# Headwise products as multiply-adds in a new channel order, and the gates of three pairs by seven products, in an mLSTM and latent-attention step

## The chip, the cores and the metric

One core of one Trainium2 chip runs the whole program. The metric is device microseconds of one execution. TensorE, VectorE (DVE), ScalarE (ACT) and GpSimd (POOL) work beside each other on SBUF and PSUM; SyncE (SP) issues nearly all DMA transfers from one queue. Everything is float32. A float32 matmul appears in the trace as two records, a transpose by the identity as one.

## What is computed

Two layers over 640 frames (512 of a new prompt, and 16 of each of 8 running streams), width 1024. The first is an mLSTM layer with 2048 channels in 4 heads of 512; the second is multi-head latent attention with 8 heads. The part that the change touches:

```python
def headwise(x, w):                       # w: 512 groups of 4 x 4
    xb = x.reshape(B, T, -1, QKV_BLOCK)
    return jnp.einsum('btgi,gio->btgo', xb, w).reshape(B, T, -1)

u = rmsnorm(x, norm_w) @ w_in             # mlstm_layer
x_in, z = u[..., :MLSTM_INNER], u[..., MLSTM_INNER:]
xc = jax.nn.silu(causal_conv(x_in, buf, conv_w, conv_b)[0])
q, k, v = headwise(xc, w_q), headwise(xc, w_k), headwise(x_in, w_v)
g = (q @ w_gates[:MLSTM_INNER] + k @ w_gates[MLSTM_INNER:2 * MLSTM_INNER]
     + v @ w_gates[2 * MLSTM_INNER:] + b_gates)
...
u = rmsnorm(x, norm_w) @ w_in             # mla_layer
gate = u[..., Q_LORA_RANK:]               # 8 tiles of 128 channels
return x + (o * jax.nn.silu(gate)) @ w_out
```

Each headwise product mixes only four neighbouring channels. Per head, k of a frame is weighed, and new states C (512 x 512) and n are formed for the prompt and for each of the 8 streams; all are outputs.

## The kernel before

**Layout.** Activations stand with channels on partitions and frames along the free dimension: a tile is 128 channels x 640 frames, an mLSTM head is four tiles (`KH`). Weights come through a ring of four slots, `ring`, 512 KB each.

**Stage A** (about 28 to 297 us) goes over the 16 channel tiles n. For each, TensorE forms x and z of the tile from the 8 tiles of the normalised input. From tile 2 on this is done by seven products in place of eight: the weights and the tokens are split in quarters, GpSimd forms four sums or differences of weights (`mixed_weights`, L2515 to L2520, 128x512 each), and the partial products are added up by VectorE (`finish_x`, `finish_z`, `middle_sums`, `lower_right`, `upper_left`) and ScalarE (`p1_kept`). TensorE works one tile ahead: while VectorE and ScalarE do the causal conv of tile n (`tap0` on ScalarE, three multiply-add taps on VectorE at L1941 and L1944) and ScalarE's SiLU, TensorE does the last z product of tile n and the products of tile n+1.

Between these products, `to_tokens` (L758) multiplies five blocks of 128 frames of x, and later of the conv's output, by a 128 x 136 matrix `basis`: 128 columns of block-diagonal 4 x 4 weights, built by GpSimd from `bdmask` (`basis_tile`), and 8 columns of gate weights. The result has frames on partitions: v from x, k from the conv's output, and the tile's share of the 8 gate rows. VectorE copies v and k out of PSUM (L1962) and adds the gates up in `gacc` (L1970); SP stores v, k and z of each tile to scratch in HBM (320 KB each). GpSimd copies the conv's output into `xc` (L2538).

**Gate rows** (about 297 to 323 us). TensorE transposes `gacc` (L869); ScalarE and VectorE form log-sigmoid, the running sums and maxima on four rows, and TensorE broadcasts the first head's row (`broadcast_first_m`, L907). Beside that, TensorE forms k and q of head 0 with channels on partitions by block-diagonal matmuls (`project_keys` L888, `project_queries` L875), and the score products (`scores`, L936) of the query blocks t = 0, 1 ahead of the broadcast and 2 to 4 behind it. SP issues four loads of old states (1024 KB each) and then, when everything stored is there (`scratch_written`), v and k of head 0.

**Heads** (about 324 to 575 us). For each head, prompt values (`prompt_values`, L1013), the stream states in eight steps (`step`: products in four column groups at L989, outer products at L1004, which VectorE adds to the old states in `update`, L2149), the prompt's new state (`prompt_c`, L1037), transposes of the normalised output (`turn`, L1022). VectorE takes statistics (`statistics`, L2122 to L2141), GpSimd the inverse roots. After step 6 of a head, `project_head` (L875, L888) forms q and k of the next, then comes step 7 and the next head's scores. ScalarE weighs k in place for the state update (`weigh_k`, L1575).

**Attention pairs** (760 to 1029 us). Four pairs of heads. While scores, maxima, exponentials and transposes go round between the engines, TensorE fills its gaps (`filler`) with the gate products of the next pair, in the first three pairs: two gate tiles of 8 k-tiles x 2 halves, 32 matmuls of 320 columns a pair (`gate_tiles`, L708).

Each engine has its own instruction stream, and the order is written out by hand; a wait names a semaphore and a count. SP's queue is in order too: a DMA behind a waiting one waits with it.

## Time and profile before

| | |
|---|---|
| median of 3 runs | 1047.45 us (1046.79 to 1049.26) |
| the profiled execution | 1046.36 us, its span 1044.6 us |
| TensorE busy | 1019.8 us (98%), 4334 matmul records |
| VectorE, ScalarE, GpSimd busy | 503.3, 259.6, 271.1 us |
| chain that ended last | TensorE 63% of the span, VectorE 4% |
| DMA | 164.20 MB, one queue, 42.5% of 16 engines' span |
| mean granted TensorE clock | 0.998 of full speed |

The span runs from the first to the last instruction; the device time is some 1.8 us longer. Matmuls are pipelined, so that the duration of one is longer than the distance from one start to the next; distances between starts are the better price. L numbers are lines of the kernel before.

### The profile page before, as it was taken

The page shows a single profiled execution, that of the slowest core. Times are in us where ns is not written, and L with a number is a line of the kernel's source. Part 1 is how long each engine was busy: PE and PEld are TensorE (multiplying, and loading weights), DVE is VectorE, ACT ScalarE, POOL GpSimd, SP SyncE. Part 2 cuts the span into 40 slices and gives each one's busy share as a digit, 9 for nine tenths or more (in the row PEclk, how much of TensorE's full clock was granted, in tenths as well). Part 3 has the DMA queues.
Part 4 walks back from the last instruction along what each step waited for, and adds up shares of the span by engine and source line. Part 5 has one row for each costly group of instructions (what it writes and reads, how often), then busy time and mean ns, then how long its engine had stood idle before and what let it go on. Part 6 is the DMA issues. An engine that isn't in the chain of part 4 may idle for free.

```text
span 1044.6 us, 12018 instructions
## 1 busy us (share of the span) xinstructions
PE 1019.8 (98%) x4334; PEld 654.8 (63%) x4334; DVE 503.3 (48%) x1134; ACT 259.6 (25%) x541; POOL 271.1 (26%) x345
## 2 busy tenths in 40 slices
PE   7999999999989999999999999999999999999998
PEld 4777777777755453444535777777766666655665
DVE  5964444444466566685665532244233333344224
ACT  3222121212154242232431000011222323243221
POOL 3552525252313234142132063311110101010110
PEclk9999999999999999999999999999999999999999
DMA  7224232423375989979798322112210111203202
GB/s 269 78 99 157 92 109 112 156 90 110 111 298 179 397 323 346 373 302 391 300 374 332 146 81 81 55 46 104 92 64 20 63 41 44 88 31 127 79 27 101
DMA packets 44464, 164.20 MB, mean 157 GB/s; under 512 B 4916, under 2 KB 8248, under 8 KB 35456
## 3 DMA queue, kind: packets, MB, share of 16 engines
q1 hardware_dynamic: 44416, 163.56, 42.5%
q8 instruction: 30, 0.49, 0.2%
q14 instruction: 18, 0.15, 0.0%
HBM read 106.32 MB, written 57.23 MB: 157 GB/s over the span
## 4 chain that ended last, share of the span: by engine, by line
PE 63%; DVE 4%; DMA 1%; POOL 1%; ACT 1%; issue 1%; SPq 0%; POOLq 0%; ACTq 0%
PE work_b L708 11%; PE work_a L708 7%; PE work_b L1246 5%; PE work_a L1037 5%; PE bank L1121 5%; PE work_a L936 3%; PE bank L1004 2%; PE work_b L1121 2%; PE work_b L989 2%; DVE arena L2149 2%; PE bank L1291 2%; PE work_a L1316 2%; PE work_a L1276 1%; PE bank L1425 1%; PE work_a L1121 1%; PE work_a L1013 1%
## 5 line engine op out<-in xcount | busy, mean ns | idle before, releaser
L2149 DVE SCALAR_TENSOR_TENSOR arena<-arena,bank 128x512 f32<-128x512 f32 x128 | 87.0, 742 | 59.3 <-PE bank L1004 59.3
L708 PE MATMUL work_b<-arena,ring 128*128 128x320 f32 x384 | 107.8, 433 | 0.0
L708 PEld LDWEIGHTS work_b<-arena,ring 128*128 128x128 f32 x384 | 71.5, 190 | 27.7
L1037 PE MATMUL work_a<-arena 128*128 128x512 f32 x128 | 64.1, 613 | 2.7 <-ACT arena L1581 2.7
L813 PE MATMUL work_a<-arena 128*128 128x320 f32 x224 | 64.9, 433 | 0.4 <-DVE arena L1916 0.4
L813 PE MATMUL work_a<-arena,ring 128*128 128x320 f32 x224 | 64.9, 432 | 0.0
L813 PE MATMUL work_b<-arena 128*128 128x320 f32 x224 | 62.7, 432 | 0.0
L708 PE MATMUL work_a<-arena,ring 128*128 128x320 f32 x192 | 55.4, 449 | 7.2 <-DMA ring<-in_stream 7.2
L2659 POOL COPY arena<-arena 32x640 f32<-32x640 f32 x20 | 16.6, 832 | 163.0 <-ACT arena L1696 156.7
L813 PEld LDWEIGHTS work_b<-arena 128*128 128x128 f32 x224 | 42.6, 190 | 17.7
L708 PEld LDWEIGHTS work_a<-arena,ring 128*128 128x128 f32 x192 | 37.9, 198 | 23.2 <-DMA ring<-in_stream 7.2
L813 PEld LDWEIGHTS work_a<-arena 128*128 128x128 f32 x224 | 41.5, 190 | 16.1 <-issue 0.6
L813 PEld LDWEIGHTS work_a<-arena,ring 128*128 128x128 f32 x224 | 41.5, 190 | 15.5
L1463 ACT ACTIVATE arena<-arena 128x128 f32<-128x128 f32 x16 | 5.0, 314 | 167.9 <-DVE arena L1876 150.4
L2581 POOL TENSOR_TENSOR xc<-arena 128x2048 f32<-128x2048 f32 (+1 forms) x8 | 23.2, 2900 | 89.4 <-DVE arena L2169 89.4
L758 PEld LDWEIGHTS bank<-arena 128*128 128x128 f32 x320 | 41.6, 190 | 7.0 <-ACT arena L1489 2.1
L758 PE MATMUL bank<-arena 128*128 (+1 forms) x320 | 42.6, 280 | 1.1 <-ACT arena L1489 1.1
L1941 DVE SCALAR_TENSOR_TENSOR arena<-arena,vec 128x512 f32<-128x512 f32 x48 | 38.1, 795 | 5.0 <-ACT arena L1470 1.6
L936 PE MATMUL work_a<-xc,arena 128*128 128x128 f32 (+3 forms) x136 | 39.2, 430 | 0.7 <-ACT arena L1516 0.7
L1013 PE MATMUL work_a<-arena 128*128 128x512 f32 x80 | 38.1, 607 | 0.0
L1037 PEld LDWEIGHTS work_a<-arena 128*128 128x128 f32 x128 | 21.1, 190 | 26.5 <-issue 26.5
L1004 PE MATMUL bank<-arena 32*128 32x512 f32 x256 | 36.5, 640 | 0.0
(336 smaller groups left out, 1795.0 us busy)
## 6 DMA issues: line engine op xcount, KB each, us to landing
ring<-in_stream SPq DMA_DIRECT2D x66, 512.0 KB, 3.4
arena<-in_c SPq DMA_DIRECT2D x32, 1024.0 KB, 9.3
out_s_c<-arena SPq DMA_DIRECT2D x32, 1024.0 KB, 6.1
arena<-in_keys SPq DMA_DIRECT2D x8, 664.0 KB, 4.2
v_scratch<-arena SPq DMA_DIRECT2D x16, 320.0 KB, 4.3
k_scratch<-arena SPq DMA_DIRECT2D x16, 320.0 KB, 4.6
z_scratch<-arena SPq DMA_DIRECT2D x16, 320.0 KB, 4.3
arena<-k_scratch SPq DMA_DIRECT2D x4, 1280.0 KB, 13.0
```

What stands on the lines that cost most here:

```text
L708: done = mm(halves(buf)[:, a, :], lhs, rhs[:, a * HALF:(a + 1) * HALF], start=first, stop=last)
L758: last = mm(bank[2 * q + t // 3][:, at:at + VG], lhs, basis[:, q, n, :], start=True, stop=True)
L813: last = mm(quarter[q], weights[:, k, :], tokens_of[:, k, :], start=fresh and k == 0, stop=k == KH - 1, skip_group_check=True)
L936: last = mm(score_bank(h, t), k_t[:, q, q0:q0 + P], xc[:, h * KH + q, q0:q0 + WID[t]], start=q == 0, stop=q == KH - 1)
L1004: mm(bank[g][:, :], kz[h % 2][rows, par, q, :], v_s[h % 2][rows], start=True, stop=True, tile_position=(32 * g, 0)).then_inc(upd_mm, 1)
L1013: last = mm(pair_bank[t % 2], weights_of(s, t), vh[:, :, s, :], start=s == 0, stop=s == t)
L1037: last = mm(pair_bank[q % 2], kh[:, q, t, :], vh[:, :, t, :], start=t == 0, stop=t == NP - 1)
L1121: last = mm(dst[:, 0:HALF], weights[:, k, :], tokens_of[:, k, :], start=k == 0, stop=k == KD - 1)
L1246: last = mm(work[1][:, w * SEQ:(w + 1) * SEQ], out_weight(t, k), og[:, k, 0:SEQ], start=k == 0, stop=k == KD - 1)
L1941: op = v.scalar_tensor_tensor(a0, xin[s][:, tap:tap + SEQ], w, a0, ALU.mult, ALU.add)
L2149: op = v.scalar_tensor_tensor(ct[s % CS][:, g, :], ct[s % CS][:, g, :], decb[:, h, b:b + 1], bank[g][:, :], ALU.mult, ALU.add)
L2581: op = g.tensor_tensor(xc[:, tiles, part], h_t[:, :, part], zh[:, :, part], ALU.mult)
```

## The change

**Channel order.** The host permutes the channels of each head: channel 4p + i of the head stands on partition p of tile i. The four channels of a group then stand on one partition in four tiles, and a headwise product is, for each output tile, a sum over four input tiles of a tile times a weight per partition. The outputs are permuted back on the host.

**v.** VectorE forms v_acc[out] += x(tile) * w for four outs a tile (`values`); in the first tile of a head it is a multiplication alone. After a head's fourth tile TensorE transposes v_acc (`turn_values`, 20 transposes), ScalarE copies it into one of three slots `v_tok`, SP stores it.

**k.** ScalarE multiplies the conv's output, now written into `xc` directly, by a weight (`weigh`), into one of four slots `part_a`; GpSimd adds it to k_acc (`sum_keys`). After four tiles SP stores k_acc (1280 KB) with channels on partitions. For the transposed use it is loaded again (`load_k`) and turned by TensorE (`turn_keys`, 20 transposes a head), and ScalarE copies and weighs it (`keep_key`).

**Keys and queries of the scores.** k_t of head 0 is formed by ScalarE and GpSimd in tiles 4 and 8 (`weigh_for_keys`, `sum_for_keys`), its queries by GpSimd in tile 12 (`new_queries`); those of a later head during the head before. `project_head`, `basis_tile` and `head_basis` are gone.

**Gates of the mLSTM.** TensorE multiplies v_acc and xc by weights 128 x 32 in four column groups at once, summing over the whole stage in bank 3 (`gates`); VectorE copies the 128 x 320 result, and four products with `gsel` give the rows.

**Gates of pairs 1 to 3.** Seven products of 4 matmuls of 320 columns (`gate_products`), with differences of tokens (`mix_gate_tokens`, four of 128x1280) and of weights (`mix_gate_weights`, four of 128x512 a pair) on GpSimd, one sum each at five places on VectorE and two copies on ScalarE.

Stage A's loops are written out tile by tile.

```diff
@@ SP, stage A and the loads of a head
-    for s in range(2):
-        for ready, out, slot, dram in ((vs_ready, v_out, vs, v_dram), (ks_ready, k_out, ks, k_dram), (zs_ready, z_out, zs, z_dram)):
-            sp.wait_ge(ready, c.next(ready))
...
+    for r in range(2):
+        load_weight(2 * n + SLOTS + r, 2 * s + r, A.fill[r])
+    sp.wait_ge(zs_ready, n + 1)
+    sp.dma_start(z_dram[n], zs[s]).then_inc(z_out[s], c.up(z_out[s], 16))
+    head, last = divmod(n, KH)
+    if last == KH - 1:
+        for t in range(TT):
+            m = TT * head + t
+            sp.wait_ge(vs_ready, m + 1)
+            sp.dma_start(v_dram[head, t], v_tok[m % len(v_tok)]).then_inc(v_out[m % len(v_tok)], 16)
+        sp.wait_ge(part_added, k_adds(n))
+        sp.dma_start(k_dram[head * KH:(head + 1) * KH].rearrange("c p n -> p c n"), k_acc).then_inc(k_out, 16)
...
-            load_kv(0)
+            load_k(0)
+            load_v(0)
@@ TensorE
-                    to_tokens(n, s, 0, xin[s])
...
+                if n % KH == KH - 1:
+                    turn_values(n // KH)
+                    gates(n // KH)
...
+            def turn_values(h):
+                pe.wait_ge(v_done, NI // HEADS * (h + 1))
+                for t in range(TT):
+                    m = TT * h + t
+                    if m >= 3:
+                        pe.wait_ge(vs_ready, m - 2)
+                    for o in range(KH):
+                        last = nc.tensor.transpose(bank[m % 3][:, o * P:(o + 1) * P], v_acc[:, o, t * P:(t + 1) * P], ident[:])
+                    last.then_inc(v_turned, 1)
+            def turn_keys(h, tiles):
+                if tiles[0] == 0:
+                    pe.wait_ge(hk_in, 16 * (h + 1))
...
+                for m in tiles:
...
+                    if h and m >= 2:
+                        pe.wait_ge(upd_done, 4 * (STEPS * h - 1) - 5 + m)
...
-            project_head(0)
             for t in range(2):
                 scores(0, t)
+            turn_keys(0, range(3))
+            pe.wait_ge(softplus, 1)
+            for t in range(2, TT):
+                if t == NP:
+                    pe.wait_ge(kn_ready, 1)
+                scores(0, t)
+            turn_keys(0, range(3, TT))
             broadcast_first_m()
...
-                    project_head(h + 1)
+                    turn_keys(h + 1, range(TT))
                     step(h, 7, t0 + 4)
@@ ScalarE
+            def weigh(dst, src, scale, parts):
+                if dst is None:
+                    k, base = adds
+                    if k - base >= len(parts):
+                        act.wait_ge(part_added, k - len(parts) + 1)
+                    dst = parts[(k - base) % len(parts)]
+                    adds[0] += 1
+                nc.scalar.activation(dst, src, ACT.Copy, scale=scale).then_inc(part_ready, c.up(part_ready))
...
+                for out in range(KH):
+                    weigh(None if i else k_acc[:, out, :], xc[:, n, :], wk_s[:, n, out:out + 1], part_a)
+                if n in KEY_TILES:
+                    weigh_for_keys(0, KEY_TILES[n], part_a)
+                if i == KH - 1:
+                    for t in range(TT):
...
+                        if m >= len(v_tok):
+                            act.wait_ge(v_out[m % len(v_tok)], 16 * (m // len(v_tok)))
+                        nc.scalar.activation(v_tok[m % len(v_tok)], bank[m % 3][:, :], ACT.Copy).then_inc(vs_ready, c.up(vs_ready))
@@ VectorE
+            def values(n, outs):
+                for out in outs:
+                    w = wv_c[:, n, out:out + 1]
+                    if n % KH == 0:
+                        op = v.tensor_scalar(v_acc[:, out, :], x, w, None, ALU.mult)
+                    else:
+                        op = v.scalar_tensor_tensor(v_acc[:, out, :], x, w, v_acc[:, out, :], ALU.mult, ALU.add)
@@ GpSimd
+            def add_part(dst, parts):
+                pool.wait_ge(part_ready, c.next(part_ready))
+                op = g.tensor_tensor(dst, dst, parts[(adds[0] - adds[1]) % len(parts)], ALU.add)
...
+                sum_keys(n)
+                if n in KEY_TILES:
+                    sum_for_keys(KEY_TILES[n], part_a)
+                if n == QUERY_TILE:
+                    new_queries(0, range(KH), q_part)
...
-                if h + 1 < HEADS:
-                    head_basis(h + 1)
+                if more:
+                    new_queries(h + 1, (3,), q_new)
+                    sum_for_keys(range(KH), part_b)
@@ TensorE, attention pairs
-                scores(0)
-                filler(4, 3)
...
+                    yield from product(low, ring[:, s0, upper, :], xb[:, upper, left], True)
+                    pe.wait_ge(pool_mixed, mixed + 2)
+                    yield from product(high, gate_w_mix[1], gate_x_mix[1], True)
+                    pe.wait_ge(prod_kept, kept + 1)
+                    yield from product(low, ring[:, s0, lower, :], xb[:, lower, left], False)
...
+                scores(0)
+                filler(8, 3)
```

## Rows read from the trace of the kernel before

**Rows 1.** Stretches: us, busy (x) of PE, PEld, DVE, ACT, POOL, PEclk, DMA share, GB/s
```profile
64.12:288.04 223.92, 223.92 (x981) 166.92 (x980) 103.28 (x273) 46.08 (x91) 82.78 (x114) 1.00 0.33 114
288.04:323.66 35.62, 30.22 (x152) 21.49 (x151) 23.53 (x61) 19.92 (x36) 6.73 (x14) 0.95 0.75 284
...
388.00:452.00 64.00, 62.99 (x303) 29.53 (x301) 42.62 (x100) 20.50 (x49) 20.00 (x31) 1.00 0.91 346
...
760.00:809.50 49.50, 49.49 (x201) 33.04 (x202) 17.19 (x53) 12.93 (x31) 3.44 (x4) 1.00 0.13 44
```

**Rows 2.** Timeline of one tile of stage A: start, us, engine, line, operation
```profile
133.68 0.36 DVE L1874 TENSOR_TENSOR arena<-work_a,arena 128x192 f32<-128x192 f32 x1 [1.66 <-PE work_a L813]
...
135.63 2.32 PE L813 MATMUL work_a<-arena,ring 128*128 128x320 f32 x8
...
137.79 1.32 PE L758 MATMUL bank<-arena 128*128 x10
...
138.94 2.32 PE L813 MATMUL work_a<-arena 128*128 128x320 f32 x8
...
151.07 0.36 DVE L1874 TENSOR_TENSOR arena<-work_a,arena 128x192 f32<-128x192 f32 x1 [1.56 <-PE work_a L813]
```

**Rows 3.** Groups by shape in 64.12 to 288.04: busy us, mean ns, idle before
```profile
L1941 DVE SCALAR_TENSOR_TENSOR arena<-arena,vec 128x512 f32<-128x512 f32 x39 | 29.2, 749 | 3.2 <-DVE arena L1944 0.8
...
L2515 POOL TENSOR_TENSOR arena<-ring 128x512 f32<-128x512 f32 x12 | 15.2, 1267 | 0.0
...
L1944 DVE SCALAR_TENSOR_TENSOR arena<-arena,vec 128x128 f32<-128x128 f32 x39 | 13.5, 346 | 0.0
...
L1489 ACT ACTIVATE arena<-arena 128x640 f32<-128x640 f32 x13 | 9.6, 737 | 14.7 <-DVE arena L1944 14.7
...
L1881 DVE TENSOR_TENSOR arena<-work_b,arena 128x320 f32<-128x320 f32 x13 | 6.4, 492 | 20.8 <-PE work_b L813 20.8
```

**Rows 4.** Two lines with 640-wide operations on SBUF: ns min/median/max, first and last start
```profile
L2668 POOL TENSOR_TENSOR arena<-arena x3: 1531/1532/2066, 707.4 to 742.4; 128x640 f32<-128x640 f32 x3
```
```profile
L1804 DVE SCALAR_TENSOR_TENSOR arena<-arena,vec,rstd x8: 875/878/2157, 702.5 to 710.1; 128x640 f32<-128x640 f32 x8
```

**Rows 5.** VectorE and GpSimd at once: timeline at 51.5, and line L2134 over the span
```profile
51.51 0.81 DVE L1868 TENSOR_TENSOR arena<-work_b,rstd 128x640 f32<-128x640 f32 x1
51.67 2.95 POOL L2525 TENSOR_TENSOR arena<-arena 128x1280 f32<-128x1280 f32 x1 [1.43 <-DVE arena L1916]
...
52.25 2.92 DVE L1941 SCALAR_TENSOR_TENSOR arena<-arena,vec 128x512 f32<-128x512 f32 x1
```
```profile
L2134 DVE TENSOR_TENSOR arena<-arena x20: 124/126/1090, 325.8 to 566.8; 128x1 f32<-128x1 f32 x20
```

**Rows 6.** The chain that ended last, in the second head: start, us, what
```profile
418.93 0.44 PE bank L1022 x4
...
430.62 1.13 PE work_a L875 x8
...
436.48 1.00 PE work_b L989 x8
```

**Rows 7.** Timeline from the last tile of stage A to the first values product
```profile
288.04 0.36 DVE L1874 TENSOR_TENSOR arena<-work_a,arena 128x192 f32<-128x192 f32 x1 [1.57 <-PE work_a L813]
...
297.24 1.25 PE L869 MATMUL bank<-ident,gacc 128*4 128x128 f32 x10 [1.20 <-DVEq L453]
...
313.81 1.12 PE L907 MATMUL bank<-arena,ones_f 4*128 4x512 f32 x2
...
316.55 4.46 PE L936 MATMUL bank<-xc,arena 128*128 128x256 f32 x16
...
321.19 1.33 ACT L1570 ACTIVATE arena<-arena 128x512 f32<-128x512 f32 x2 [0.83 <-DMA arena<-k_scratch]
...
323.66 1.10 PE L1013 MATMUL work_a<-arena 128*128 128x512 f32 x2
```

**Rows 8.** DMA in 294.6 to 321.3: queue, packets, MB, share of 16 engines
```profile
q1 hardware_dynamic: 3325, 9.54, 94.3%
```

More of the change, by code:

```diff
@@ L59 @@
 SLOTS = 4
+VS = 3
 CS = 4
@@ L307, in program @@
         top[0] = 0
+        vh = take(NP, HD)
+        assert top[0] == KH * KH * P
+        k_t = take(KH, T)
+        q_t = take(KH, P)
         kh = take(KH, TT, P)
-        vh = take(KH, NP, P)
-        v_s = [take(KH, P) for _ in range(2)]
+        v_s = [take(HD) for _ in range(2)]
         kz_at = top[0]
@@ L379, in program @@
         keys_c = take(KEYS_W)
+        gate_w_mix = [take(KH, P) for _ in range(2)]
+        gate_u4 = take(HALF)
         k0 = top[0]
@@ new lines, in gates @@
+            def gates(h):
+                if h == 0:
+                    pe.wait_ge(basis_ready, 1)
+                for q, tiles in enumerate((v_acc, xc[:, h * KH:(h + 1) * KH])):
+                    if q:
+                        pe.wait_ge(xc_ready, KH * (h + 1))
+                    for k in range(0, KH, 2):
+                        for r in range(4):
+                            i, a = k + r // 2, r % 2
+                            last = mm(bank[3][32 * r:32 * r + 32, 0:HALF], gate_w[:, q, h * KH + i, :],
+                                      tiles[:, i, a * HALF:(a + 1) * HALF], start=h == 0 and q == 0 and k == 0,
+                                      stop=h == HEADS - 1 and q == 1 and k == KH - 2, skip_group_check=True, tile_position=(0, 32 * r))
+                last.then_inc(v_turned, 1)
@@ L971, in _ @@
             op.then_inc(G.bfill[0], c.up(G.bfill[0]))
-            for t in range(2, TT):
-                scores(0, t)
             def stream_own(h):
@@ L1339, in filler @@
+                gates = gate_products()
                 def filler(n_gate, n_out):
                     if p < PAIRS - 1:
-                        gate_tiles([next(gates) for _ in range(n_gate)])
+                        for _ in range(n_gate):
+                            next(gates)
                     else:
@@ L1494, in _ @@
-            stage_a(0)
-            c.rounds(NI // 2 - 2, stage_a, first=1)
-            stage_a(NI // 2 - 1, end=True)
+            act.wait_ge(const_in, c.all(const_in, ahead=5, step=16))
+            adds = [0, 0]
+            def weigh(dst, src, scale, parts):
[6 more added lines that the diff above has]
+                nc.scalar.activation(dst, src, ACT.Copy, scale=scale).then_inc(part_ready, c.up(part_ready))
@@ L1497, in _ @@
+            for n in range(NI):
+                stage_a(n)
             leave(c)
@@ L1982, in _ @@
-            stage_a(0)
-            c.rounds(NI // 2 - 2, stage_a, first=1)
-            stage_a(NI // 2 - 1, end=True)
+                        lower_right(s)
+                dve.wait_ge(A.free[0], c.all(A.free[0]))
+                if n >= 2:
+                    dve.wait_ge(prod_sum, c.all(prod_sum))
+                if n:
+                    dve.wait_ge(v_done, n)
+                    dve.wait_ge(dve_own, c.all(dve_own))
+                values(n, [0, 1])
+                if n >= 2 and not last_x:
+                    finish_z(s)
```

836 lines of the change are left out of this document (441 added, 395 removed).

## Prediction

> **What bounds the kernel now.** I read the stretches first: from the third channel tile to the sixteenth [rows 1] TensorE is busy in every microsecond, and it is the bound there. In the stretch of the gate rows (288.04 to 323.66) it is busy 30 of 36 us; in a head of the mLSTM (388 to 452) 63 of 64, with DMA at 91%; in a pair of attention heads 49.49 of 49.50. The timeline of one tile [rows 2] gives the unit prices. Four products of 320 columns (eight records) take 2.16 us from start to start, the five products `to_tokens` 1.16 us. A tile has seven groups of the first kind and two of the second: 7 x 2.15 + 2 x 1.16 = 17.4 us, which is the pitch of L1874 in [rows 2]. So what leaves TensorE in this stage is gained one for one, as long as VectorE, GpSimd, ScalarE and the queue keep their places.
>
> Then I read what the others need per operation [rows 3, 4], what happens when VectorE and GpSimd meet [rows 5], the chain in a head [rows 6], and the way from the end of stage A to the first values product [rows 7], with the DMA queue beside it [rows 8].
>
> **Stage A up to the last tile.** Removed: two `to_tokens` of 1.16 us in each of 15 tiles, 34.8 us. Added, for three heads: 20 transposes (a group of four is 0.44 us in [rows 6], so 2.2 us) and `gates`, 16 products in four column groups. L989 in [rows 6] is four such products of 512 columns, side by side, in 1.00 us; at 320 columns four groups take 2.5 us. 3 x 4.7 = 14.1. TensorE alone would be 34.8 - 14.1 = 20.7 us earlier at the start of the last tile, and its 13 tiles from 64.12 on would need 223.9 - 13 x 2.32 + 14.1 = 207.8 us.
>
> The moved work goes to VectorE (four multiply-adds of 128x640 a tile, `values`) and GpSimd (`sum_keys`: four adds of 128x640 in three tiles of four, six more in tiles 4 and 8, seven operations of 512 for the queries in tile 12), fed by ScalarE. ScalarE has room: it is busy 46.08 us in 13 tiles [rows 1], 3.5 each, and its 640-wide operation is 0.74 [rows 3]: four more make 6.5 us a tile, and the twelve of tiles 4 and 8 still fit in 15. Alone, GpSimd needs 4 x 1.27 + 4 x 1.53 = 11.2 us of 15.06, and VectorE 4 x 0.88 + 3 x (0.75 + 0.35) + 6 x 0.49 = 9.8 [rows 3, 4].
>
> But they don't run side by side. In [rows 5] GpSimd's subtraction runs from 51.67 to 54.62, and the multiply-add that VectorE begins at 52.25 takes 2.92 us in place of 0.75: it ended after GpSimd's. The operation with an operand in PSUM right before it ran at its usual 0.81. L2134, a one-element operation on two SBUF operands, is 0.13 as a rule and 1.09 at most. So an operation of VectorE with two SBUF operands and one of GpSimd exclude each other. The maxima of [rows 4] say for how long: the 640-wide add of 1.53 made a multiply-add of 0.88 take 2.16, so it held the path some 1.28 us (0.25 less than it lasts, and VectorE's 0.08 less: an operation's start overlaps the one before), and itself took 2.07. Both `values` and the conv taps are of this kind.
>
> What the path must carry in those 13 tiles, by held times: 48 weight mixes x 1.02 = 49, 52 adds x 1.28 = 67, seven query operations 7, 40 `values` x 0.80 = 32, 39 taps x (0.67 + 0.28) = 37: 192 us of TensorE's 207.8, 92%. Two serial engines don't fill a common path to 92% without making each other late. I follow the tile. In a usual one GpSimd's adds run into the first four microseconds of the next and its mixes start at about 6, so the taps meet three or four operations, end at 8 to 11, and the sums that TensorE needs (u2 by 12.9, the lower right by 15.06) just make it. After tiles 4 and 8 GpSimd works without a break, six taps each wait some 1.1 us, and the next fourth product starts about 5 us late: 2 x 5. Tile 12's queries, and `turn_values` waiting for the last of `values` (due about 10.8, done about 12), cost about 4 more. In the first two tiles TensorE would wait for x_mix, which is VectorE's, so 3 us of the removed products are not gained. Together 17 of the 20.7 go: **-4 us**. Bounds: -21 if every collision falls into a gap, +12 if each delays the chain.
>
> For the two-operand operations the Trainium skill (SBUF - State Buffer, Who interferes with whom) says the same, that VectorE's second SBUF input and GpSimd share a path held exclusively, and it holds it for the whole instruction. By that, the listed durations count whole; what this makes is the second rival.
>
> **End of stage A to the first values product.** I count from L1874 of the last tile (288.04) [rows 7]. Before: the transposed gates start at 9.2, the broadcast L907 at 25.8, prompt values at 35.6. After: the conv ends at 7.9, ScalarE's SiLU's and four weighted copies at 12.3, and then its five copies of turned values; the fourth and fifth wait for the store of the first and second slot (three slots), so it leaves at 18.1. TensorE is done at 16.7. SP issues the store of k_acc (1280 KB) after the last of these, at 18.5; then 4 MB of old states; and `load_k(0)` when the store has landed. The queue gives no way past: in [rows 8] it was full at 94%, 9.54 MB in 26.7 us. From 18.5 the rest of v (0.26), k out (1.31), states (4.19) and k in (1.31 MB) at 0.385 MB/us are 18.4 us: keys at 37.4. Before, the landing was at 321.19 - 288.04 = 33.2 (ScalarE's first use of them), and only ScalarE's stream keys waited. Now TensorE does: `turn_keys` (1.3), scores 2 to 4 (two of them take 4.46 in [rows 7], where they run after the broadcast; with the small last one 5.3), `turn_keys` (0.9) and the last copy (0.7) stand ahead of the broadcast: 45.7, and 9.7 us later prompt values at 55.4: 55.4 - 35.6 = **+19.8 us**. The projections of keys and queries that are removed there free nothing. The lower bound takes the keys as early enough: leaving 9 later and 1 more for the four selection products makes the gate chain 10 late: +10. Upper: +24, if the queue is slower or the granted clock, already 0.95 in this stretch [rows 1], falls in TensorE's longer idle time.
>
> **Three head changes.** Queries and keys took from 430.62 to 436.48, 5.86 us [rows 6]; 20 transposes take 2.2: -3.7 each if TensorE is last. But `turn_keys` waits, from its third tile, for VectorE's update of step 6, and that stands behind `add_skip`, four two-operand operations that now meet GpSimd's twelve key adds (409 to 432): about 5 us later, so the transposes end near 436.5 as before. And in the chain after `small_sums`, where VectorE's statistics are last (L2134 of [rows 5]), `new_queries` of 1.27 us each now run between the roots: 1 to 2 us a head. **+5**, bounds -9 and +9. DMA at 91% [rows 1] leaves only 5 us a head anyway.
>
> **Gates of pairs.** 28 instead of 32 products of 320 columns (0.54 us) in each of three pairs: -2.15 x 3 = **-6.5 us**. The sums and copies fall where both engines wait (VectorE is busy 17, ScalarE 13, GpSimd 3 of 49.5 us [rows 1]), and the token mixes end before the first pair, at about 761. At worst a wait of 0.5 a pair: -5.
>
> **Sum**: -4 + 19.8 + 5 - 6.5 = +14.3 on the profiled execution's 1046.36 (span 1044.6, 1.8 around it; the median of the runs is 1.1 higher): 1060.7, so 1061.
>
> **Rivals.** (1) Faster: GpSimd's adds fall into VectorE's gaps and TensorE stays the bound in stage A. Then -21 there, +14 at the gate rows, -3 in the heads, -6.5: 1030. For it: only the last sums of a tile bind, and both engines are idle a quarter of the tile or more when each is summed alone. It decides if TensorE's idle time between tiles 2 and 15 stays under about 5 us. 0.24. (2) The path is held whole: 48 x 1.27 + 52 x 1.53 + 7 x 1.27 + 40 x 0.88 + 39 x 1.10 = 228 us, 20 more than TensorE's 207.8, and with the 6 of the first tiles and `turn_values` stage A is 6 us longer than before: 1071. For it: 0.88 to 2.16 was measured once only. 0.15. (3) The keys aren't last: the queue has drained (stores of stage A are spread), and the gate chain binds: +10 in place of +19.8: 1051. 0.13. (4) Savings and losses cancel to within 0.2% (about what a measurement of this kernel can tell from no change): 0.03. The forecast keeps 0.45.
>
> **How the numbers follow.** The forecast's own range is 1052 to 1070. Slower: 0.45 + 0.15 + 0.13 = 0.73; same 0.03; faster 0.24. The range reaches down to 1034, which leaves out half of rival 1, and up to 1080, between rival 2 and both upper bounds.
>
> **What would show it.** In the profile after: idle time of TensorE ahead of last and fourth products, above all after tiles 4 and 8, with multiply-adds of 1.5 to 2.2 us on VectorE; the broadcast behind `turn_keys`, whose releaser is the DMA of k_scratch; key adds at 1.5 to 2.3 us on GpSimd; pairs at 47.2 us. The prediction is wrong if the stretch of the 13 tiles is near 208 us, or if the keys land before the gate chain is done.

## The result, and the profile of the changed kernel

The change makes the kernel slower: 1076.79 us (median of 4 runs, 1075.31 to 1079.08) beside 1047.12 for the kernel before on the same chip, a ratio of 1.0286 (95% interval 1.0265 to 1.0308), +29.7 us. The forecast was +14. The profiled execution took 1076.58 us, its span is 1074.8. L numbers below are lines of the changed kernel unless an experiment is named.

I cut the spans where the prediction cut its sum: at the `finish_x` of tile 2 (64.12 before, 64.6 now), at that of the last tile, at the first values product and at pair 0. The stretches of the changed kernel (columns as in [rows 1]) and, below them, the last two stretches of the kernel before:

```profile
64.12:298.40 234.28, 217.19 (x879) 151.15 (x878) 179.95 (x207) 103.67 (x174) 178.12 (x134) 0.96 0.31 111
298.40:355.70 57.30, 34.34 (x178) 24.07 (x178) 24.60 (x53) 27.23 (x47) 13.85 (x12) 0.78 0.51 194
355.70:794.75 439.05, 426.80 (x1841) 242.20 (x1842) 242.07 (x430) 124.19 (x240) 198.20 (x177) 0.99 0.60 228
794.75:1074.80 280.05, 273.62 (x1106) 175.82 (x1106) 115.27 (x302) 80.85 (x183) 46.26 (x52) 1.00 0.18 64
```
```profile
323.66:760.01 436.35, 429.36 (x1855) 244.98 (x1854) 228.29 (x443) 94.33 (x206) 123.37 (x140) 1.00 0.61 229
760.01:1044.60 284.59, 279.75 (x1130) 180.85 (x1130) 100.14 (x287) 82.44 (x183) 26.52 (x39) 1.00 0.18 63
```

| term | forecast | measured |
|---|---|---|
| up to the last tile's `finish_x` | -4 | 298.40 - 288.04 = +10.4 |
| from there to the first values product | +19.8 | 57.30 - 35.62 = +21.7 |
| from there to pair 0 (the three head changes lie here) | +5 | 439.05 - 436.35 = +2.7 |
| pairs and end | -6.5 | 280.05 - 284.59 = -4.5 |
| sum | +14.3 | +30.3 |

The first row is where it went: VectorE and GpSimd are both busy for about 180 of 234 us (103 and 83 in [rows 1]), and TensorE, which had no idle time at all, is idle for 17 and at 0.96 of its clock. By shape (busy us, mean ns, idle before), the operations of the 13 tiles:

```profile
L2601 POOL TENSOR_TENSOR arena<-arena 128x640 f32<-128x640 f32 x53 | 92.2, 1763 | 20.7 <-ACT arena L1503 20.1
...
L1999 DVE SCALAR_TENSOR_TENSOR arena<-arena 128x640 f32<-128x640 f32 x40 | 57.9, 1468 | 0.3
L2028 DVE SCALAR_TENSOR_TENSOR arena<-arena,vec 128x512 f32<-128x512 f32 x39 | 50.7, 1300 | 0.9
...
L2031 DVE SCALAR_TENSOR_TENSOR arena<-arena,vec 128x128 f32<-128x128 f32 x39 | 33.8, 865 | 0.0
```

The same taps took 0.75 and 0.35 in [rows 3]: now 1.30 and 0.87. What that does to TensorE, in its waits from 64 to 300 us (in total, times, longest):

```profile
PE bank L806 <- DVE arena L1999: 14.6, 3, 4.9
PE work_b L845 <- DVE arena L1968: 1.6, 2, 1.1
```

So the sums of the tiles come in time, nearly always; what is late is the last of a head's `values`, for which `turn_values` (L806) waits 4.8 to 5.0 us in each of four heads (the fourth stands behind the last `finish_x`). And the wait costs more than it lasts. The stretches from within the first one on (TensorE busy, granted clock, DMA share, GB/s):

```profile
92.00:96.00 4.00, 0.68 (x4) 0.82 0.01 4
96.00:100.00 4.00, 4.00 (x22) 0.50 0.45 167
100.00:104.00 4.00, 4.00 (x37) 0.83 0.89 331
```

TensorE stood still from 90.4 to 95.3. Then its 20 transposes and first gate products ran mostly at half the clock (a granted clock of 0.50, the lower level of 1.2 GHz), the transposes 4.5 us in place of the 2.2 reckoned.

From the last tile on (start, us, engine, line; the idle time and its releaser in brackets):

```profile
308.63 4.69 PE L806 MATMUL bank<-ident,arena 128*128 128x128 f32 x20 [5.01 <-DVE arena L1999]
...
317.84 2.31 PE L901 MATMUL bank<-arena,gsel 128*4 128x320 f32 x8 [2.23 <-DVE arena L2065]
...
336.77 1.12 PE L918 MATMUL work_b<-ident,arena 128*128 128x128 f32 x4 [9.52 <-DMA arena<-k_scratch]
...
345.22 1.09 PE L924 MATMUL bank<-arena,ones_f 4*128 4x512 f32 x2 [0.83 <-ACT arena L1588]
...
355.70 2.05 PE L1034 MATMUL work_a<-arena 128*128 128x512 f32 x2
```

Counted from 298.40: keys at 38.4 (forecast 37.4), broadcast at 46.8 (45.7), prompt values at 57.3 (55.4). `turn_keys` waits for the DMA of k_scratch, 9.5 us.

### The profile page after: what moved, and what is told of

Read it like the earlier page. It is cut to its first block, busy times and chain, and to the rows that moved or that the text cites. A ratio compares the mean times of both kernels' runs of the same rounds, so it can differ in the third digit from the quotient of the medians.

```text
span 1074.8 us, 11431 instructions
## 1 busy us (share of the span) xinstructions
PE 1003.9 (93%) x4180; PEld 628.9 (59%) x4180; DVE 614.3 (57%) x1050; ACT 358.7 (33%) x677; POOL 466.8 (43%) x404
## 4 chain that ended last, share of the span: by engine, by line
PE 55%; DVE 7%; DMA 3%; POOL 2%; ACT 1%; issue 1%; SPq 0%; POOLq 0%; ACTq 0%
PE work_a L736 6%; PE work_b L1267 5%; PE work_b L736 5%; PE bank L1142 5%; PE work_b L1351 4%; PE work_a L1058 4%; PE work_a L953 3%; PE work_b L1142 2%; DVE arena L2212 2%; PE bank L1025 2%; PE work_b L1010 2%; DMA out_p_c<-arena 2%; PE work_a L1337 2%; PE bank L1312 2%; PE work_a L1297 1%; PE bank L1464 1%
## 5 line engine op out<-in xcount | busy, mean ns | idle before, releaser
L2601 POOL TENSOR_TENSOR arena<-arena 128x640 f32<-128x640 f32 x96 | 152.9, 1608 | 50.4 <-ACT arena L1503 47.8
L845 PE MATMUL work_a<-arena 128*128 128x320 f32 x224 | 66.8, 442 | 6.6 <-DVE arena L1958 3.7
L1058 PE MATMUL work_a<-arena 128*128 128x512 f32 x128 | 66.7, 635 | 4.9 <-ACT arena L1646 4.9
L1999 DVE SCALAR_TENSOR_TENSOR arena<-arena 128x640 f32<-128x640 f32 x48 | 68.6, 1451 | 0.4
L2028 DVE SCALAR_TENSOR_TENSOR arena<-arena,vec 128x512 f32<-128x512 f32 x48 | 59.4, 1237 | 1.7 <-ACT arena L1525 0.6
L845 PEld LDWEIGHTS work_a<-arena 128*128 128x128 f32 x224 | 43.2, 194 | 26.2 <-DVE arena L1958 5.1
L736 PE MATMUL work_b<-arena,ring 128*128 128x320 f32 x192 | 52.8, 432 | 0.0
L1503 ACT ACTIVATE arena<-xc,wkq 128x640 f32<-128x640 f32 x64 | 49.1, 824 | 9.5 <-POOL arena L2601 9.5
L1503 ACT ACTIVATE arena<-xc,wk_s 128x640 f32<-128x640 f32 x64 | 47.8, 818 | 0.5
L736 PEld LDWEIGHTS work_b<-arena,ring 128*128 128x128 f32 x192 | 36.5, 190 | 15.2
L1710 ACT ACTIVATE arena<-arena 128x640 f32<-128x640 f32 x8 | 5.9, 737 | 100.2 <-DVE arena L2311 75.6
L1034 PE MATMUL work_a<-arena 128*128 128x512 f32 x80 | 39.1, 619 | 0.0
L1058 PEld LDWEIGHTS work_a<-arena 128*128 128x128 f32 x128 | 21.9, 196 | 29.2 <-issue 29.2
```

The lines of the kernel that those rows point to most:

```text
L736: done = mm(halves(buf)[:, a, :], lhs, rhs[:, a * HALF:(a + 1) * HALF], start=first, stop=last)
L845: last = mm(quarter[q], weights[:, k, :], tokens_of[:, k, :], start=fresh and k == 0, stop=k == KH - 1, skip_group_check=True)
L1058: last = mm(pair_bank[q % 2], kh[:, q, t, :], vh[:, t, :], start=t == 0, stop=t == NP - 1)
L1503: nc.scalar.activation(dst, src, ACT.Copy, scale=scale).then_inc(part_ready, c.up(part_ready))
L1999: op = v.scalar_tensor_tensor(v_acc[:, out, :], x, w, v_acc[:, out, :], ALU.mult, ALU.add)
L2028: op = v.scalar_tensor_tensor(a0, xin[s][:, tap:tap + SEQ], w, a0, ALU.mult, ALU.add)
```

## What was left to explain

Theory 1, the prediction's with a larger price: VectorE and GpSimd exclude each other on a common path, and that makes `values` late. Rivals: VectorE has too much work by itself; `turn_values` merely stands at a bad place of TensorE's order; ScalarE's weighed copies are late; what is lost is mostly clock. And if it is the path: does its total count, as the prediction reckoned, or the way in which the two engines share it?

Each run below stands beside runs of the kernel before on its own chip, and its ratio is to those. "By the ratios" is the difference of its ratio and the 1.0286 of the changed kernel (or of two runs' ratios, where two are compared), times 1047 us.

## Experiments: what makes stage A late

**The key adds out of the way.** All that touch `part_a` (64 adds) made one column wide.

```diff
+                part = parts[(adds[0] - adds[1]) % len(parts)]
+                if parts is part_a:
+                    dst, part = dst[:, 0:1], part[:, 0:1]
+                op = g.tensor_tensor(dst, dst, part, ALU.add)
```

> The changed kernel with the key adds of stage A one column wide in place of 640 (k is left unsummed but for that column); ScalarE still weighs every part. Theory 1 (common path): `values` at 0.88 us, taps that meet only the four weight mixes, the waits ahead of the transposes of v under 1 us; TensorE's pace in stage A, -25 us, about 1052. Theory 2 (VectorE's own work, or ScalarE's weighed copies, make stage A late): less than -5 us.

1051.88 us, ratio 1.0040 (1.0024 to 1.0055): -26 by the ratios. The 13 tiles, 67.0 to 276.3, took 209.3 us, where the prediction had 207.8 for TensorE alone. VectorE's durations went back to those of an operation alone in the median, 0.89 for `values` (second fence: ns min/median/max over the run) and 0.75 for the taps, but not on average over the 13 tiles (third fence): 18 of the 40 `values` took 1.2 us or more, most of them beside weight mixes.

```profile
67.00:276.30 209.30, 208.78 (x877) 145.67 (x876) 133.27 (x208) 104.65 (x174) 94.21 (x133) 1.00 0.35 124
```
```profile
L1999 DVE SCALAR_TENSOR_TENSOR arena<-arena x48: 873/887/3052, 51.5 to 284.8; 128x640 f32<-128x640 f32 x48
```
```profile
L1999 DVE SCALAR_TENSOR_TENSOR arena<-arena 128x640 f32<-128x640 f32 x40 | 48.0, 1220 | 0.3
```

ScalarE still did all its work (104.65 us busy), and VectorE all of its own: both rivals fall. This run takes 84 us of GpSimd's own busy time away too (178 to 94), so it can't tell yet whether GpSimd makes VectorE late or is late itself; the shorter adds below can. It also shows that with a stage A at TensorE's pace the change would still not be faster than the kernel before, because of what follows.

**`values` with one operand.** A multiplication alone in every tile, so that v is left unsummed.

```diff
-                    if n % KH == 0:
+                    if True:
                         op = v.tensor_scalar(v_acc[:, out, :], x, w, None, ALU.mult)
```

> The changed kernel with every operation of `values` a multiplication alone (one operand in SBUF besides the weight column), so that v is left unsummed; VectorE still has as many operations of 128x640, and GpSimd the same adds. Theory 1 (VectorE and GpSimd exclude each other on a common path when VectorE reads two operands from SBUF): the 40 operations go from 1.47 us to 0.86, the waits of TensorE ahead of the transposes of v from 4.9 us to about 2.5, and the time falls by 10 to 15 us, to about 1064. Theory 2 (VectorE has too much work in a tile, alone): durations and waits stay, and the time within 2 us of 1077.

1062.71 us, ratio 1.0147 (1.0130 to 1.0165): -15 by the ratios, in the range of theory 1, but `values` went to 1.23 us on average, not to the 0.86 expected there. By shape in 63.1 to 285.6 us of this run:

```profile
L1997 DVE TENSOR_SCALAR arena<-arena 128x640 f32<-128x640 f32 x52 | 62.7, 1226 | 0.5
L2028 DVE SCALAR_TENSOR_TENSOR arena<-arena,vec 128x512 f32<-128x512 f32 x39 | 45.0, 1155 | 0.9
```

The multiplication does meet GpSimd: its shortest is 0.54 us, its median 1.21 and its longest 2.72. It waits like the others and is only shorter when nothing holds it up. So "two operands in SBUF" was too narrow a rule. The Trainium skill (SBUF - State Buffer, Who interferes with whom) says that `tensor_scalar` too can contend with GpSimd, in a fast mode that uses both of VectorE's port pairs; 0.54 us against 0.87 for the two-operand form of that size fits such a mode.

**`turn_values` later.** Transposes and gate products of heads 0 to 2 behind the next tile's fourth product, ScalarE's copies and the stores of v after them, `values` of that tile behind its taps.

```diff
                 else:
                     fourth_product(n, s)
+                if n and n % KH == 0:
+                    turn_values(n // KH - 1)
+                    gates(n // KH - 1)
```

> The changed kernel with the transposes of v and the gate products of heads 0 to 2 put behind the fourth product of the next tile (ScalarE's copies and the stores of v follow them, VectorE forms the next `values` after the taps); the last head's stay. Collisions on the common path stay as they are. Theory 1 (a wait that stands in TensorE's order at a place where the work is not yet due to be done; collisions themselves are within the slack of a tile): three waits of 4.9 us and the half clock behind them go, about -20 us, 1057. Theory 2 (VectorE as a whole is late, so that the wait only moves to the next product that needs a sum): waits of 3 to 5 us ahead of L845's products, under -6 us, 1071 or more.

1075.53 us, ratio 1.0269 (1.0252 to 1.0286): -1.8 by the ratios. This is theory 2. The three waits of 4.9 us are gone, the clock of the stretch is 0.99, and TensorE is idle for 17 us of the 232.3 of its 13 tiles, as much as before, in pieces of at most 2.3 us, partly for ScalarE (its waits, 30 to 300 us):

```profile
PE work_a L853 <- DVE arena L1971: 7.2, 8, 1.4
PE work_a L853 <- ACT arena L1555: 5.9, 3, 2.3
PE work_b L853 <- DVE arena L1981: 3.8, 4, 1.3
```

VectorE, busy 188.7 us of them, is late as a whole; the long wait was only the place where it showed.

**The waits filled.** Unused products into a free bank ahead of each wait for `values`, and ahead of that for the keys.

```diff
+                fill(bank[TT * h % 3][:, 0:HALF], 9)
                 pe.wait_ge(v_done, NI // HEADS * (h + 1))
```

> The changed kernel, with nine products of 320 columns (4.9 us) into a free bank ahead of each of the four waits of TensorE for `values`, and seventeen (9.2 us) ahead of its wait for the keys of head 0; nothing else moves, and the results of these products are not used. Theory 1 (the waits cost more than they last, because TensorE runs at half its clock after them): the waits are as long as before, now filled, and what follows runs at full clock: 20 transposes in 2.3 us in place of 4.5, the gates in 2.6 in place of 3.2, scores and transposes behind the keys some 3 us faster. But one run has shown that three waits of 4.9 us can be taken away and VectorE, busy for 189 of 232 us, is then late elsewhere; so of these 3 us a head only the last head's and the keys' are sure: -6 us from those, -6 more if the three others count: 1065 to 1071. Theory 2 (the clock holds nothing up, since the next sums of VectorE are what TensorE waits for anyway): 0 to +2 us, 1077 to 1079.

1072.02 us, ratio 1.0222 (1.0206 to 1.0238): -6.7 by the ratios, in the lower half of theory 1. The transposes that took 4.5 us, in this run (2.7 us of work and 0.4 of waiting for ScalarE):

```profile
92.84 5.01 PE L799 MATMUL bank<-arena 128*128 128x320 f32 x18
97.80 1.53 PE L811 MATMUL bank<-ident,arena 128*128 128x128 f32 x12
99.69 1.14 PE L811 MATMUL bank<-ident,arena 128*128 128x128 f32 x8 [0.36 <-ACT arena L1567]
```

Stage A's 13 tiles (66.8 to 296.2) are 4.4 us shorter than the 233.8 of the changed kernel. So the half clock behind the waits is worth some 4 us there and 7 in all, and the lateness itself the rest. Some 3 of the 7 lie behind the wait for the keys: the first values product comes 54.4 us after the last `finish_x` in place of 57.3.

**Shorter adds.** Each key add of stage A as two of 320 columns.

```diff
+                if parts is part_a:
+                    g.tensor_tensor(dst[:, 0:HALF], dst[:, 0:HALF], part[:, 0:HALF], ALU.add).then_inc(pool_own, c.up(pool_own))
+                    dst, part = dst[:, HALF:T], part[:, HALF:T]
+                op = g.tensor_tensor(dst, dst, part, ALU.add)
```

> The changed kernel with each of the 64 key adds of stage A as two of 320 columns. From the rows of 1.27 us for 512 and 1.53 for 640 columns an operation of GpSimd has 0.23 us that do not shrink, so this adds 0.23 us for each, 15 us of GpSimd's and of the common path's time. Theory 1 (what holds VectorE up is that each of its operations waits out one of GpSimd's, so shorter ones help): taps and `values` fall from 1.3 and 1.47 us to some 0.9 and 1.1, and the time falls by 5 to 10 us, 1070. Theory 2 (the path is full: one of the two engines holds it for 208 of 234 us, and only its total counts): 5 to 12 us slower, 1085.

1064.05 us, ratio 1.0149 (1.0134 to 1.0164): -14 by the ratios, although GpSimd has more to do: it is busy 191.5 us of the 218.7 that the 13 tiles took, in place of 177.6 of 233.8. (The profiled execution, 1059.9 us, was the fastest of the four, some 4 us ahead of the others.) The taps fell from 1.30 and 0.87 us to 1.07 and 0.80 on average, and TensorE's four waits for `values` from 19.6 to 14.1 us; `values` itself stayed at 1.43, where theory 1 had 1.1. GpSimd was not what was late, since more work on it made the kernel faster. The timelines show how the path is shared. First the changed kernel, the taps of a tile beside weight mixes; then this run, beside half adds (L2603, L2605):

```profile
144.79 1.38 DVE L2031 SCALAR_TENSOR_TENSOR arena<-arena,vec 128x128 f32<-128x128 f32 x1
145.97 1.36 POOL L2591 TENSOR_TENSOR arena<-ring 128x512 f32<-128x512 f32 x1
146.21 1.67 DVE L2028 SCALAR_TENSOR_TENSOR arena<-arena,vec 128x512 f32<-128x512 f32 x1
147.28 1.71 POOL L2593 TENSOR_TENSOR arena<-arena,ring 128x512 f32<-128x512 f32 x1
147.79 1.35 DVE L2031 SCALAR_TENSOR_TENSOR arena<-arena,vec 128x128 f32<-128x128 f32 x1
```
```profile
152.84 0.95 DVE L2031 SCALAR_TENSOR_TENSOR arena<-arena,vec 128x128 f32<-128x128 f32 x1
153.60 0.91 POOL L2605 TENSOR_TENSOR arena<-arena 128x320 f32<-128x320 f32 x1
153.82 1.23 DVE L2028 SCALAR_TENSOR_TENSOR arena<-arena,vec 128x512 f32<-128x512 f32 x1
154.47 1.31 POOL L2603 TENSOR_TENSOR arena<-arena 128x320 f32<-128x320 f32 x1
154.98 0.94 DVE L2031 SCALAR_TENSOR_TENSOR arena<-arena,vec 128x128 f32<-128x128 f32 x1
```

They take turns, one operation each. Counted over the 13 tiles of the changed kernel, 73 of VectorE's 130 multiply-adds and multiplications saw an operation of GpSimd end while they were under way, and none saw two; of GpSimd's 108 operations with two operands 66 saw one of VectorE's end, and none two. With the halved adds it is 101 of 130 and 89 of 158, again none with two. A tap of 128 columns that needs 0.35 us is there for 1.35 beside mixes of 512 columns and for 0.95 beside adds of 320: it waits out the other's operation. Whoever has the shorter operations gets less of the path in a turn.

**Shorter `values`.** The mirror image: each operation of `values` as two of 320 columns, the adds left whole.

```diff
+                    for a in range(2):
+                        half = slice(a * HALF, (a + 1) * HALF)
...
+                            op = v.scalar_tensor_tensor(v_acc[:, out, half], x[:, half], w, v_acc[:, out, half], ALU.mult, ALU.add)
```

> The changed kernel with every operation of `values` (128x640) as two of 320 columns, 64 more operations of VectorE; GpSimd's adds stay 640 wide. Theory 1 (on the common path the two engines take turns, an operation each, so that every operation of VectorE that meets GpSimd waits out one of its operations, however short it is itself): a value's mean of 1.47 us is 0.88 and 0.59 of waiting; as two it waits twice, some 0.6 us more each, 24 us more of VectorE's time in the 13 tiles, and the time rises by 8 to 15 us, 1085 to 1092. Theory 2 (only the total held on the path counts): 0.1 us more for each, up to 4 us, 1077 to 1081.

1090.46 us, ratio 1.0415 (1.0399 to 1.0430): +13.5 by the ratios. Groups by shape in its 13 tiles (65.8 to 312.4, 246.6 us in place of 233.8):

```profile
L2603 POOL TENSOR_TENSOR arena<-arena 128x640 f32<-128x640 f32 x53 | 86.0, 1646 | 30.5 <-ACT arena L1503 29.9
L2001 DVE SCALAR_TENSOR_TENSOR arena<-arena 128x320 f32<-128x320 f32 x80 | 80.1, 1051 | 0.3
```

Two halves are 2.10 us in place of one of 1.47: +0.63, as expected from turns, and the turns are again one operation each. Between them, the last two runs move the time by 28 us with the same numbers added and multiplied.

**Adds in four parts.** Four of 160 columns.

```diff
+                    cuts, wide = 4, T // 4
+                    for a in range(cuts - 1):
+                        at = slice(a * wide, (a + 1) * wide)
+                        g.tensor_tensor(dst[:, at], dst[:, at], part[:, at], ALU.add).then_inc(pool_own, c.up(pool_own))
+                    dst, part = dst[:, T - wide:T], part[:, T - wide:T]
```

> The changed kernel with each of the 64 key adds of stage A as four of 160 columns, where two of 320 gave -12.7 us. Theory 1 (turns): what VectorE waits in a turn halves again, to about 0.35 us, but GpSimd has 0.2 us more for each of 192 operations and gives VectorE a turn between all of them, so GpSimd becomes late: tiles 4 and 8 with 16 adds need some 45 us of the path's four tiles less than before for nothing; between -10 and +3 against 1064 of the two halves, most likely 1066. Theory 2 (the gain of the halves came from an earlier end of each add, so that ScalarE's parts flow better): the gain goes on, below 1060.

1080.20 us, ratio 1.0306 (1.0288 to 1.0324): 16 us slower than the halves, far outside my range for it. VectorE gained as in theory 1 (taps 0.95 and 0.65 us on average), but GpSimd is now the one that is late, and TensorE waits for its weight mixes (L2595) too (TensorE's waits, 30 to 360 us):

```profile
PE bank L806 <- DVE arena L1999: 9.8, 4, 6.7
PE work_a L845 <- POOL arena L2595: 7.3, 5, 2.5
```

A quarter of an add is 0.65 us on average, four are 2.6 in place of 1.76. The direction of theory 1 holds; I took too little for GpSimd's turns. The turns are not strict here: 3 of 130 operations of VectorE waited out two or three of GpSimd's.

## Experiments: the other terms, and a version that is faster

**Keys first.** `load_k(0)` and `load_v(0)` ahead of the old states, once head 0's own stores have landed.

```diff
-            for s in range(CS):
-                load_c(s)
-            sp.wait_ge(stage_left, 4)
-            scratch_written(sp)
...
+            sp.wait_ge(stage_left, 4)
+            sp.wait_ge(k_out, 16)
...
             load_k(0)
             load_v(0)
+            for s in range(CS):
+                load_c(s)
+            scratch_written(sp)
```

> The changed kernel with SP's loads of the keys and values of head 0 issued when all engines have left stage A and head 0's stores have landed, ahead of the four loads of old states (4 MB) in place of behind them. Theory 1 (the prediction's: the states stand between the store of k_acc and the keys, and the keys are last): the transposes of the keys start at 28 to 29 us after the last `finish_x` in place of 38.4, then the gate chain and they bind together, the broadcast at 37 in place of 46.8: -10 us, 1067. Theory 2 (the queue is the bound from here through the heads, so that what is loaded later is missed later): the first values product is 10 us earlier, but the updates of the first head wait for states, and at the end 4 us or less are left, 1073.

1066.34 us, ratio 1.0166 (1.0145 to 1.0188): -12.6 by the ratios. `turn_keys` starts 29.7 us after the last `finish_x` (300.0) and no longer waits, the broadcast is at 36.4 and prompt values at 46.4, 10.9 earlier than in the changed kernel. Theory 1: the round trip behind 4 MB of states was half of the loss at the gate rows, and nothing is missed later. The other half is the gate chain, whose first products on TensorE start at 18.8, where the transposes of the gates started at 9.2 in [rows 7].

**The gates of the pairs alone**, in the kernel before: the hunks of the change on `gate_products`, `gate_sums`, `mix_gate_tokens` and `mix_gate_weights`, and nothing else.

```diff
-                filler(4, 3)
+                filler(8, 3)
...
+            mix_gate_tokens()
...
+                if p < PAIRS - 1:
+                    mix_gate_weights(p)
```

> The kernel before with one part of the change alone: the gates of pairs 1 to 3 by seven products. Theory 1 (the sum read from the trace of the changed kernel, where the stretch from the first products of pair 0 to the end is 4.5 us shorter): 1042.6 us, -4.5. Theory 2 (the prediction's term, 12 fewer products of 0.54 us, no new wait): -6.5 us, 1040.6. Theory 3 (the four subtractions of 128x1280 or the weight mixes hold VectorE up in the pairs): -2 us or less.

1042.78 us, ratio 0.9947 (0.9934 to 0.9961): faster than both kernels, by 5.5 us of the kernel before. The trace has it like that of the whole change: from the first products of pair 0 (761.90) to the end (1041.8) 279.9 us in place of 284.6; they start 1.9 us later than in the profiled execution before, for no reason that is shown. In each of the first three pairs a wait of 0.5 us is new, 1.5 us in all (pair 0, TensorE; columns of the timeline):

```profile
773.38 1.88 PE L1275 MATMUL work_a<-arena,xc 128*128 128x512 f32 x4
775.75 1.16 PE L1282 MATMUL work_b<-xc 128*128 128x128 f32 x8 [0.48 <-DVE xc L2382]
```

**Three edits together**: half adds and keys first as above, and this:

```diff
+                if last_x:
+                    pe.wait_ge(v_done, NI)
+                    gates(n // KH)
+                    turn_values(n // KH)
```

> The changed kernel with three edits together: the key adds of stage A as two of 320 columns (-12.7 us when alone), the keys and values of head 0 loaded ahead of the old states (-10.5 when alone), and in the last tile the gate products ahead of the transposes of v (the gate chain 2.5 to 4.5 us earlier). If the three lie on one path one after the other, the sum is 1076.8 - 12.7 - 10.5 - 3.5 = 1050. If the queue of DMA is the next bound behind the keys, 1055. Below 1047 it would beat the kernel before.

1054.43 us, ratio 1.0073 (1.0060 to 1.0087), where the ratios of the first two edits alone would add up to 1.003. So the third edit gave nothing. Behind the last `finish_x` (286.9) the transposes now start at 16.0 in place of 11.9 with the half adds alone, and the first products of the gate rows (last row below) at 21.9 in place of 20.4:

```profile
302.92 2.94 PE L812 MATMUL bank<-ident,arena 128*128 128x128 f32 x20
308.77 2.31 PE L907 MATMUL bank<-arena,gsel 128*4 128x320 f32 x8 [2.92 <-DVE arena L2071]
```

In the next run VectorE's copy of the gate rows waits for the gate products alone.

```diff
-            dve.wait_ge(v_turned, (TT + 1) * HEADS)
+            dve.wait_ge(v_turned, (TT + 1) * (HEADS - 1) + 1)
```

> The three edits together as before, and VectorE's copy of the gate rows waits for the gate products of the last head alone (in the run before it also waited for the transposes behind them, 2.9 us, so that the third edit gave nothing). Theory 1 (the gate chain is last at the broadcast, now that the keys come early): -2.5 to -3, 1051.5. Theory 2 (the keys or the copies of ScalarE are last at the broadcast): -1 or less.

1055.11 us, ratio 1.0072 (1.0046 to 1.0097): no gain. My reading of the run before was wrong. What is last ahead of the gate rows is ScalarE's last two copies of turned values, which wait for a slot; all engines leave stage A together behind them, and VectorE's copy of the gate rows stands behind that. Later transposes make those copies later, so the third edit moved the gate chain the wrong way, by some 1.5 us. Half adds and keys first without it were not run together. The rows, from this run (start, us, engine, line):

```profile
307.90 1.27 ACT L1566 ACTIVATE arena<-bank 128x512 f32<-128x512 f32 x2 [1.16 <-DMA v_scratch<-arena]
309.24 0.49 DVE L2071 COPY arena<-bank 128x320 f32<-128x320 f32 x1 [9.66 <-ACTq L475]
```

**Halved weight mixes** besides.

```diff
+                def mixed(dst, x, y, op):
+                    h0, h1 = slice(0, KH // 2), slice(KH // 2, KH)
+                    g.tensor_tensor(dst[:, h0], x[:, h0], y[:, h0], op).then_inc(pool_own, c.up(pool_own))
+                    g.tensor_tensor(dst[:, h1], x[:, h1], y[:, h1], op).then_inc(pool_mixed, c.up(pool_mixed))
```

> The same, with GpSimd's four weight mixes of a tile (128x512) as two halves each besides. Theory 1 (turns on the common path): the taps that meet mixes wait some 0.5 us less each, six a tile, for 0.2 us more of GpSimd for each mix; VectorE has the values of the last tile of a head ready earlier by 1.5 to 2.5 us, and TensorE's waits for them (2 to 7 us each, four) shrink by that: -4 to -8 us beside the run without it, 1045. Theory 2 (GpSimd, whose adds must be done before the next tile's, is the later one by now, as with adds in four parts): no gain or up to +8.

1059.36 us, ratio 1.0120 (1.0095 to 1.0146): slower by 5 us than without, theory 2. The 13 tiles took 226.2 us (63.7 to 289.9) in place of 221.5, and TensorE waits for the weight mixes, as with adds in four parts (5.6 us, 5 times). Shorter operations on GpSimd help while VectorE is the later one, and by here it isn't.

## Why the prediction was wrong, point by point

The sign was right and the size was half of what came (+14 against +29.7 us). By its own steps:

- **The step that failed is the size of stage A**, "Together 17 of the 20.7 go: -4 us". Measured: +10.4, so 31 of the 20.7 go, inside the stated bound of +12. The two ends of the reckoning held: TensorE alone needs 209.3 us for the 13 tiles (207.8 forecast), and the mechanism is the path of VectorE and GpSimd. Above those 207.8 the 13 tiles took 26 us more: 17 in which TensorE was idle, 14.6 of them ahead of `turn_values`, and 9 in which it was busy for longer, some 6 of them in the 60 transposes behind the three waits (12.9 us, 6.6 reckoned). The price of lateness was wrong in three ways. I put the stalls after tiles 4 and 8; they stand at the end of every head, four of 4.9 us. I allowed `turn_values` a lateness of about 1 us (10.8 against 12). And I gave a wait its length only, while the clock behind the waits is worth 7 us over the whole kernel.
- **Why the lateness was underrated.** I summed held times to 92% of a serial resource and guessed what the last 8% do. From the timelines of the changed kernel, one or other engine has such an operation under way for 206 us of the 233.8 (the union of their rows, waiting included; the 208 in the expectation above is a little high, and the 192 forecast were held times). But with turns of one operation each, the total doesn't say who is late: the halved adds gave 14 us back, and the union is 205 us of their 218.7. The row that would have said it is in [rows 5], a tap of 0.75 that ends after a subtraction of 2.95: every tap pays for GpSimd's operation, a 128-column one as much as a 640-column one. VectorE has six taps and four `values` in a tile, and the mean extra wait is 0.55 us for each of them (taps 0.55 and 0.52, `values` 0.59 over 39, 39 and 40): 65 us in 13 tiles.
- **Front**: forecast +19.8, measured +21.7; the keys, the broadcast and prompt values each within 2 us of their times. Taking the loads out of the way of the states gave the 10 us that the lower bound had. In part the closeness is luck. The parts listed for the keys add up to 18.5 + 18.4 = 36.9, not 37.4; the rate of 0.385 MB/us is above the 9.54 MB in 26.7 us of [rows 8] (0.357), with which the keys come at 38.3 (38.4 measured); and some 3 us of the measured term are clock, which the sum had at nothing.
- **Heads**: +5 forecast, +2.7 measured. What the three head changes did singly was not taken apart, so the mechanism of this term is not shown.
- **Gates of pairs**: -6.5 forecast, -4.5 in the trace and -5.5 by the ratio of the part alone; the token mixes end 1 us behind the first product of pair 0 (795.8 against 794.75), not ahead of it, and a wait of 0.5 us is new in each of three pairs, which is the prediction's own worst case of -5.
- **Rivals.** The first (GpSimd falls into gaps) is refuted by the 17 us of TensorE's idle time. The second said +6 for stage A with the path held for 228 us; its size is nearer to what came than mine, but the union of 206 us and the gain from shorter adds speak against its reason. The third (the keys aren't last) is refuted by TensorE's 9.5 us of waiting for them.

What stays open: how much of the 28 us in which neither engine used the path could be had by another order of their work, and whether a stage A at 209 us can be reached with all adds in place. The best complete version of the change that was run is at 1.007 of the kernel before; the gates of the pairs alone are at 0.995.

## What to carry to other kernels

When work is moved from TensorE to VectorE and GpSimd together, count operations that meet, not microseconds: each operation of VectorE on the common path that meets one of GpSimd's waits it out. Make the operations of the engine with slack shorter, leave those of the engine that others wait for whole, and stop when the slack is used up. Price a wait of TensorE with the clock behind it, and look at what stands ahead of a load in its queue before sending data through memory and back.

## What the hardware showed that was not expected

- VectorE and GpSimd alternated operation by operation on SBUF operands, with no exception among 130 operations of VectorE in the changed kernel's 13 tiles and 3 where GpSimd's adds were cut in four. A 128x128 multiply-add: 0.35 us alone, 0.95 beside 320-column adds, 1.35 beside 512-column ones. Adds of 640 columns in two parts: -14 us; multiply-adds of 640 columns in two parts: +13.5 us.
- A multiplication by a column with a single 128x640 operand takes 0.54 us alone, against 0.87 for the two-operand form, and waits for GpSimd too (median 1.21, longest 2.72).
- After 4.9 us without work TensorE's granted clock was 0.50 (in 96 to 100 us), and 20 transposes took 4.5 us in place of 2.7 with the wait filled.
